# Pairing the level scores of the first mixer behind two rows of the next head's products

## The chip, the cores and the metric

The kernel runs on one core of a Trainium2 chip. The metric is device time in microseconds (us) of one launch. The engines are TensorE (PE: matmuls, PEld: its weight loads), VectorE (DVE), ScalarE (ACT), GpSimd (POOL) and SyncE (SP, which issues the weight loads). Each engine works through its own queue in order and waits on semaphores for the others.

## The reference, cut to what matters

Two blocks of a transformer-like model on 512 tokens of width 1024 in float32: mixers (a gated linear recurrence, sparse attention, dense attention, a long convolution), each followed by a gated feed-forward part. The change lies in the first mixer, which has 8 heads of 128:

```python
def hgrn2_mixer(x, w_in, w_out, gate_norm, lower_bound):
    proj = x @ w_in
    q, f, i, g = jnp.split(proj, 4, axis=-1)
    forget = lb + (1.0 - lb) * jax.nn.sigmoid(f32)
    log_f = jnp.log(jnp.maximum(forget, TINY))
    k = (1.0 - lb) * jax.nn.sigmoid(-f32)
    ...
        decay = jnp.where(causal, jnp.exp(jnp.where(causal, diff, 0.0)), 0.0)
        scores = jnp.einsum('bhtd,bhsd,bhtsd->bhts', qb, kb, decay)
        o = jnp.einsum('bhts,bhsv->bhtv', scores, ib) + ...
    ...
    o = o * lax.rsqrt(jnp.mean(o * o, axis=-1, keepdims=True) + EPS) * gate_norm
    o = o * jax.nn.silu(g)
    return o.reshape(B, L, D_MODEL) @ w_out
```

So for each head: gates and queries from a product with the input, decayed scores between every query and every earlier key, the scores times the values, a norm over the head, a gate.

## The kernel before, in words

The program is written out by hand, one queue for each engine, with semaphores between them. In the first mixer the decays are not built as differences. The 512 tokens are cut in levels n = 0 to 8: at level n a block of 2^n keys meets the next block of 2^n queries, and the decay between them splits in a product over one side and a product over the other. For every head and level VectorE makes one tile `H.E` of decayed keys and queries (`level`, L2181) and updates the running products for the next level (L2189). TensorE multiplies that tile with itself (`scores`). The result in PSUM is collected into `H.S` by mask (VectorE, L2203 and L2206, for levels 0 to 3 and the diagonal) or by copies (ScalarE, L1588, for levels 4 to 6, and L1594 into `H.SO` for 7 and 8).

The order of one head's ten scores is `ORDER = [0, 1, 2, 3, None, 4, 5, 6, 7, 8]`, where `None` is the diagonal, a product of keys and queries without a level. There are four level tiles (`NE = 4`, so level n of a head may be written once the score four levels back has read its tile) and four PSUM banks for scores, `LEVEL_BANKS`, taken in turn.

Between its scores TensorE runs the products of the next head, gate and query, by rows: `head(h + 1, (row,))` is one row k of 8 of the weight tile. It has 6 matmuls of 128x128 by 128x512, since every float32 product is made of three products of rounded parts (L573, L574, L575) and there are two column groups. These rows are cover for VectorE's work. Row 0 of the head after next is done after score 8, then come `values(h)` (L910 to L918), and the next head begins with row 1. So heads 1 to 6 have seven rows and ten scores. The sums of squares of the head before (`head_sums`, L631) stand behind score 3 and the spread of its norm (`head_spread`, L932) behind score 6. Head 7 has no next head: from its sixth score on, rows of the output projection (`mixed`) stand between the scores, which need parts made by ScalarE (L1579) and GpSimd (L2719).

VectorE's queue for a head, in order: clamp of the forget gate (L2226), levels 0, 1, 2 each with its update, collect score 0, level 3, collect 1, collect 2, the low part of a weight tile (L1975), level 4, collect 3, the reciprocal for the norm of the head before (L1988), level 5, collect the diagonal, level 6, level 7, the head before's output (L2213), level 8, the head before's normalisation (L2218), the next head's clamp. That is `LAG = 2`: a score is collected two levels behind the level being made. ScalarE makes the next head's gates and query (L1550 to L1561) after it has collected score 4, and copies the weight tile's high part (L1404) at the end of a head.

Of the kernel before, what the change touches and what calls it, by code (L numbers as in the profile page):

```python
# [17 lines left out]
NT = D // 128  # L18
# [15 lines left out]
LEVEL_BANKS = (2, 4, 5, 6)  # L34
ORDER = [0, 1, 2, 3, None, 4, 5, 6, 7, 8]
# [28 lines left out]
def level_slot(h, n):  # L64

    return (9 * h + n) % NE
# [190 lines left out]
class Signals:  # L257
# [6 lines left out]
    def mark(self, name, *events, by=1):  # L264
        self.total[name] = self.total.get(name, 0) + by
        for event in events:
            self.value[event] = (name, self.total[name])
        self.newest[name.split("_")[0]] = (name, self.total[name])
        return (self.handles[name] if self.handles else None), by
# [4 lines left out]
    def at(self, *event):  # L274
        if self.counted is None:
            return None, 0
        name, value = self.counted[event]
        return self.handles[name], value
# [86 lines left out]
def build(nc, A, out):  # L365
    ctx = ExitStack()
    with ctx:
# [190 lines left out]
        def pe_program(pe):  # L558
# [3 lines left out]
            def wait_bank(b):  # L562
                for event in freed[b] or ():
                    pe.wait_ge(*at(*event))
# [17 lines left out]
            def project(sem, key, banks, done, then, tile=None, ready=None, rows=None, cols=(0, 1)):  # L582

                it = items[key]
                a, b = w_views(it)
                tile = tile or (lambda k: (hh[:, k, :], hl[:, k, :]))
                rows = rows or range(it["kt"])
                wait_weights(key)
                if rows[0] == 0:
                    for j in cols:  # L590
                        wait_bank(banks[j])
                for k in rows:
                    for event in ready(k):
                        pe.wait_ge(*at(*event))
                    for j in cols:
                        bk = banks[j]
                        c = slice(128 * j, 128 * j + 128)
                        last = k == it["kt"] - 1
                        m = product(ps[bk][:, :], [((a[:, k, c], b[:, k, c]), tile(k))], k == 0, last)
                        if last:  # L600
                            m.then_inc(*mark(sem, done[j], *([("used", key)] if j == 1 else [])))
                            freed[bk] = then[j]
# [236 lines left out]
            def hgrn():  # L839
# [4 lines left out]
                for c in range(2):  # L844
# [3 lines left out]
                    for part in range(2):  # L848
# [3 lines left out]
                        for i in range(4):  # L852
                            k = 4 * part + i
# [15 lines left out]
                def head(h, rows):  # L869
                    project("pe_hgrn", ("hgrn", "fq", h), (0, 1), [("f_mm", h), ("q_mm", h)], [[("k_raw", h)], [("q", h)]], ready=ready, rows=rows)  # L870

                def scores(h, n, bk):
                    wait_bank(bk)
                    i = h % 2
                    if n is None:
                        pe.wait_ge(*at("q", h))
                        pe.wait_ge(*at("k", h))
                        a_, b_ = H.K[i], H.Q[i]
                    else:
                        pe.wait_ge(*at("level", h, n))  # L880
                        a_ = b_ = H.E[level_slot(h, n)]
                    if n == 8:
                        for t in range(2):
                            m = pe.matmul(ps[bk][:, 256 * t:256 * t + 256], a_[:, 128 * t:128 * t + 128], b_[:, 256:512], start=True, stop=True)
                    elif n == 7:
                        for t in range(2):
                            m = pe.matmul(ps[bk][:, 128 * t:128 * t + 128], a_[:, 256 * t:256 * t + 128],
                                          b_[:, 256 * t + 128:256 * t + 256], start=True, stop=True)
                    elif n == 6:
                        for t in range(4):  # L890
                            keys, queries = slice(128 * t, 128 * t + 64), slice(128 * t + 64, 128 * t + 128)
                            m = pe.matmul(ps[bk][0:64, queries], a_[:, keys], b_[:, queries], start=True, stop=True)
                    else:
                        for t in range(4):
                            for e in range(2):
                                c = slice(128 * t + 64 * e, 128 * t + 64 * e + 64)
                                m = pe.matmul(ps[bk][64 * e:64 * e + 64, c], a_[:, c], b_[:, c], start=True, stop=True, skip_group_check=True)
                    m.then_inc(*mark("pe_level", ("scores", h, n)))
                    freed[bk] = [("collect", h, n)]

                def values(h):
                    i, hc = h % 2, slice(128 * h, 128 * h + 128)
                    wait_bank(OB)
                    for c in range(2):
                        for tt in range(4):
                            pe.wait_ge(*at("i", c, tt))
                    pe.wait_ge(*at("collect", h, 7))
                    pe.wait_ge(*at("collect", h, 8))
                    for s in range(2):
                        pe.matmul(ps[OB][:, 256:512], H.I[:, s, hc], H.SO[:, 256 * s:256 * s + 256], start=s == 0, stop=False, **kw)  # L910
                    pe.matmul(ps[OB][:, 128:256], H.I[:, 0, hc], H.SO[:, 512:640], start=False, stop=False, **kw)
                    pe.matmul(ps[OB][:, 384:512], H.I[:, 2, hc], H.SO[:, 640:768], start=False, stop=False, **kw).then_inc(
                        *mark("pe_hgrn", ("far_used", h)))
                    pe.wait_ge(*at("collect", h, None))
                    pe.wait_ge(*at("collect", h, 6))
                    for tt in range(4):
                        c = slice(128 * tt, 128 * tt + 128)
                        m = pe.matmul(ps[OB][:, c], H.I[:, tt, hc], H.S[i][:, c], start=False, stop=tt == 3, **kw)  # L918
                    m.then_inc(*mark("pe_hgrn", ("o_mm", h)))
                    freed[OB] = [("o", h)]  # L920

                def head_sums(h):
                    wait_bank(HB)
                    pe.wait_ge(*at("o2", h))
                    sums(HB, sq[h % 2], True, True).then_inc(*mark("pe_hgrn", ("o2_sum", h)))

                    freed[HB] = [("rms", "head", h)]

                def head_spread(h):
                    pe.wait_ge(*at("diagonal", h))  # L930
                    wait_bank(HB)
                    pe.matmul(ps[HB][:, :], ones[:, :], rb[1][:, :], start=True, stop=True).then_inc(*mark("pe_stat", ("spread", "head", h)))  # L932
                    freed[HB] = [("m", h)]

                def mixed(n, rows):

                    project("pe_hgrn", ("hgrn", "out", n), ((0, 1), (4, 5))[n], None, None, ready=mix, rows=rows)

                head(0, None)
                n_level = 0  # L940
                for h in range(8):
                    for i, n in enumerate(ORDER):

                        row = i + (h > 0)
                        if h < 7 and row < NT:
                            head(h + 1, (row,))
                        elif h == 7 and i >= 5:
                            mixed(0, (i - 5,))
                        scores(h, n, LEVEL_BANKS[n_level % 4])
                        n_level += 1  # L950
                        if i == 3 and h:
                            head_sums(h - 1)
                        if i == 7 and h:
                            head_spread(h - 1)
                    if h < 6:
                        head(h + 2, (0,))
                    elif h == 7:
                        mixed(0, (5,))
                    values(h)
# [412 lines left out]
            end("pe", "begin")  # L1372
            normalise("hgrn", 0)
            hgrn()
            ffn(0)
            dsa()
# [1591 lines left out]
```

## Time and profile before

| | |
|---|---|
| median of 3 runs | 2756.11 us (2754.98 to 2756.7) |
| the profiled execution, its own time | 2755.34 us |
| its span, first to last instruction | 2753.4 us |
| granted TensorE clock, mean | 0.996 |
| TensorE, VectorE, ScalarE, GpSimd busy | 2704.0, 1732.6, 1031.1, 136.5 us |

The profile gives for every instruction its start and its duration. Durations of TensorE's matmuls are modelled and overlap, so the distance from one start to the next is what an instruction costs there. "Idle before" is the time for which an engine stood still, with the instruction that released it as inferred from the semaphores.

### The profile page before, as it was taken

Reading aid. Unit: us, or ns where it says so; the run is one execution under the profiler, and the core shown is the slowest. Engines: PE = TensorE matmul, PEld = TensorE weight load, DVE = VectorE, ACT = ScalarE, POOL = GpSimd, SP = SyncE. Lnnn points to the kernel's source line nnn. Section 1 sums busy time; section 2 is a strip of 40 time slices with the busy share of each in tenths; the row PEclk is TensorE's granted clock in tenths of the full one; section 3 lists DMA queues with packets and bytes.
Section 4 is the critical chain, followed back from the end, with each engine's and each line's share of the span. In section 5 each row is a group of like instructions: output and inputs, shape, how many; then the busy total and the mean of one; then the engine's idle time right before and its main releaser. Section 6 shows DMA issues by size and latency. Waiting matters only on the chain.

```text
span 2753.4 us, 36096 instructions
## 1 busy us (share of the span) xinstructions
PE 2704.0 (98%) x14724; PEld 2180.2 (79%) x14724; DVE 1732.6 (63%) x2551; ACT 1031.1 (37%) x1496; POOL 136.5 (5%) x171
## 2 busy tenths in 40 slices
PE   8999899999999999999899999999999999999999
PEld 6777688888876788888675788888887888888888
DVE  4388677465587477565657567575664888643434
ACT  4345444232435444232436543232332222432323
POOL 0000200000034200000003200000000000000000
PEclk9999999999999999999999999999999999999999
DMA  5432134343312134343310036454331111332221
GB/s 172 117 75 66 62 127 153 123 145 96 102 62 77 54 127 153 123 145 96 101 62 16 32 119 200 152 188 134 112 120 58 35 35 35 105 120 93 92 85 54
DMA packets 260572, 276.87 MB, mean 101 GB/s; under 512 B 23799, under 2 KB 227063, under 8 KB 260408
## 3 DMA queue, kind: packets, MB, share of 16 engines
q1 hardware_dynamic: 230216, 219.51, 25.3%
q10 hardware_dynamic: 30192, 55.05, 6.3%
q8 instruction: 118, 1.93, 0.3%
q14 instruction: 46, 0.38, 0.0%
HBM read 267.19 MB, written 7.34 MB: 100 GB/s over the span
## 4 chain that ended last, share of the span: by engine, by line
PE 83%; DVE 4%; ACT 2%; issue 1%; ACTq 0%; DVEq 0%
PE ps L573 23%; PE ps L575 23%; PE ps L574 23%; PE ps L1286 3%; PE ps L1318 2%; PE ps L1045 2%; PE ps L1062 1%; PE ps L1243 1%; PE ps L1264 1%; PE ps L1079 1%; PE ps L1151 1%; ACT sb L1404 1%; PE ps L1130 1%; PE ps L631 0%; PE ps L1196 0%
## 5 line engine op out<-in xcount | busy, mean ns | idle before, releaser
L573 PE MATMUL ps<-sb 128*128 128x512 f32 (+2 forms) x3396 | 1276.1, 376 | 10.6 <-DVE sb L2008 2.5
L574 PE MATMUL ps<-sb 128*128 128x512 f32 (+2 forms) x3396 | 1254.8, 369 | 0.0
L575 PE MATMUL ps<-sb 128*128 128x512 f32 (+2 forms) x3396 | 1254.7, 369 | 0.0
L573 PEld LDWEIGHTS ps<-sb 128*128 128x128 f32 x3396 | 640.1, 188 | 139.4 <-issue 26.5
L575 PEld LDWEIGHTS ps<-sb 128*128 128x128 f32 x3396 | 640.2, 189 | 109.7
L574 PEld LDWEIGHTS ps<-sb 128*128 128x128 f32 x3396 | 640.5, 189 | 106.7 <-issue 1.9
L1975 DVE TENSOR_TENSOR sb<-sb 128x2048 fp32r<-128x2048 f32 (+2 forms) x187 | 417.8, 2234 | 318.4 <-ACT sb L1404 318.3
L1404 ACT ACTIVATE sb<-sb 128x2048 fp32r<-128x2048 f32 (+1 forms) x195 | 363.2, 1862 | 268.7 <-PE ps L575 267.2
L2261 DVE SCALAR_TENSOR_TENSOR sb<-ps,sb 128x511 f32<-128x511 f32 (+1 forms) x264 | 193.5, 747 | 125.8 <-ACT sb L1659 120.6
L1659 ACT ACTIVATE sb<-ps,sb 128x512 f32<-128x512 f32 x132 | 96.1, 778 | 273.5 <-PE ps L575 270.4
L2297 DVE SCALAR_TENSOR_TENSOR sb<-sb 128x512 f32<-128x512 f32 x168 | 126.0, 750 | 13.9 <-DVE sb L2297 0.9
L1690 ACT ACTIVATE sb<-sb 128x512 fp32r<-128x512 f32 x88 | 55.3, 633 | 210.2 <-DVE sb L2319 125.9
L1286 PE MATMUL ps<-sb 128*128 128x256 f32 x512 | 113.5, 380 | 1.3 <-ACT sb L1875 1.3
L1286 PEld LDWEIGHTS ps<-sb 128*128 128x128 f32 x512 | 97.0, 190 | 17.9 <-issue 3.3
L2762 POOL TENSOR_SCALAR sb<-sb 128x512 f32<-128x512 f32 (+3 forms) x128 | 77.1, 616 | 628.0 <-DVE sb L2351 628.0
L2120 DVE SCALAR_TENSOR_TENSOR sb<-ps,sb 128x512 f32<-128x512 f32 x56 | 40.4, 750 | 105.7 <-PE ps L575 105.7
L2118 DVE TENSOR_TENSOR sb<-sb,ps 128x512 f32<-128x512 f32 x58 | 39.1, 685 | 87.2 <-PE ps L575 87.2
L1675 ACT ACTIVATE sb<-sb 128x512 f32<-128x512 f32 x88 | 55.3, 632 | 93.9 <-DVE sb L2261 93.8
L1473 ACT ACTIVATE sb<-sb 128x512 f32<-128x512 f32 x58 | 36.3, 643 | 119.0 <-DVE sb L2079 50.7
L1984 DVE TENSOR_TENSOR sb<-sb 128x512 fp32r<-128x512 f32 x97 | 65.4, 689 | 5.7 <-ACT sb L1889 1.3
L2725 POOL TENSOR_TENSOR sb<-sb 128x2048 fp32r<-128x2048 f32 x8 | 36.9, 4607 | 503.7 <-ACT sb L1404 503.7
L1988 DVE RECIPROCAL sb<-sb 64x128 f32<-64x128 f32 (+4 forms) x36 | 29.7, 825 | 50.3 <-ACT sb L1412 25.3
(239 smaller groups left out, 2202.5 us busy)
## 6 DMA issues: line engine op xcount, KB each, us to landing
sb<-in_ffn_w_up SPq DMA_DIRECT2D x88, 1024.0 KB, 4.9
sb<-in_ada_w ACTq DMA_DIRECT2D x192, 256.0 KB, 3.2
sb<-in_ffn_w_down SPq DMA_DIRECT2D x32, 1024.0 KB, 5.0
sb<-in_ffn_w_down SPq DMA_DIRECT2D x16, 768.0 KB, 4.3
sb<-in_hy_w_in SPq DMA_DIRECT2D x12, 1024.0 KB, 4.9
sb<-in_hgrn_w_in SPq DMA_DIRECT2D x8, 1024.0 KB, 6.3
sb<-in_hgrn_w_in SPq DMA_DIRECT2D x16, 512.0 KB, 4.6
sb<-in_dsa_w_in SPq DMA_DIRECT2D x6, 1024.0 KB, 5.1
```

The source lines that it names most:

```text
L573: pe.matmul(o, al, bh, start=f, stop=False, **kw)
L574: pe.matmul(o, ah, bl, start=False, stop=False, **kw)
L575: m = pe.matmul(o, ah, bh, start=False, stop=l, **kw)
L1286: m = pe.matmul(o, fwm[:, kt, cols], sdz(i, sc)[:, 2 * half + kt, :], start=kt == 0, stop=kt == 1)
L1404: act.activation(wh[w][:, 0:n], raw[it["r"]][:, 0:n], ACTF.Copy).then_inc(*mark("act_hi", ("hi", it["key"])))
L1659: act.activation(dst[:, :], ps[b][:, :], ACTF.Identity, bias=bias(tile), scale=wt(offset, tile)).then_inc(*mark("act_ffn", (name + "_0", n ...
L1675: act.activation(N.sg[i][:, :], N.yg[i][:, :], ACTF.Silu).then_inc(*mark("act_ffn", ("silu", n, t)))
L1975: dve.tensor_tensor(wl[w][:, 0:n], raw[it["r"]][:, 0:n], wh[w][:, 0:n].bitcast(F), SUB).then_inc(*mark("dve_lo", ("lo", it["key"])))
L1984: dve.tensor_tensor(dst, src, high.bitcast(F), SUB).then_inc(*mark(sem, (*name, "lo")))
L2261: dve.scalar_tensor_tensor(o, i, cv[0](tap, tile), o, MUL, ADD).then_inc(*mark("dve_ffn", (name, n, tile) if last else (name + "_1", n, ti ...
L2297: m = dve.scalar_tensor_tensor(a, w[:, :], cact[:, f:f + 1], a, MUL, ADD)
L2762: pool.tensor_scalar(P, P, M.rs[:, c:c + 1], 1.0, MUL, MUL).then_inc(*mark(f"pool_{stage}", ("scaled", stage, u, e)))
```

## The change

The ten scores of a head are taken two at a time. In front of a pair stand the rows that stood in front of each of the two before. Head_sums stays behind score 3, head_spread behind score 6. No instruction is added or taken out, and only TensorE's queue changes.

```diff
                 for h in range(8):
-                    for i, n in enumerate(ORDER):
-
-                        row = i + (h > 0)
-                        if h < 7 and row < NT:
-                            head(h + 1, (row,))
-                        elif h == 7 and i >= 5:
-                            mixed(0, (i - 5,))
-                        scores(h, n, LEVEL_BANKS[n_level % 4])
-                        n_level += 1
-                        if i == 3 and h:
+                    for i in range(0, len(ORDER), 2):
+                        for k in (i, i + 1):
+                            row = k + (h > 0)
+                            if h < 7 and row < NT:
+                                head(h + 1, (row,))
+                            elif h == 7 and k >= 5:
+                                mixed(0, (k - 5,))
+                        for n in ORDER[i:i + 2]:
+                            scores(h, n, LEVEL_BANKS[n_level % 4])
+                            n_level += 1
+                        if i == 2 and h:
                             head_sums(h - 1)
-                        if i == 7 and h:
+                        if i == 6 and h:
                             head_spread(h - 1)
                     if h < 6:
                         head(h + 2, (0,))
```

## Rows read from the trace of the kernel before

**Rows 1.** The page: busy us (share of the span) xinstructions

```profile
PE 2704.0 (98%) x14724; PEld 2180.2 (79%) x14724; DVE 1732.6 (63%) x2551; ACT 1031.1 (37%) x1496; POOL 136.5 (5%) x171
```

**Rows 2.** Windows of heads 1 and 6: length, busy by engine, clock, DMA

```profile
152.00:174.90 22.90, 22.28 (x205) 16.68 (x204) 19.64 (x28) 12.48 (x25) 0.53 (x1) 1.00 0.34 75
...
243.50:266.40 22.90, 22.27 (x205) 16.68 (x204) 19.83 (x28) 12.48 (x25) 0.53 (x1) 1.00 0.15 47
```

**Rows 3.** Timeline, TensorE, head 2: start us, us, engine line op [idle before <-releaser]

```profile
174.91 0.48 PE L573 MATMUL ps<-sb 128*128 128x512 f32 x1
...
176.48 0.69 PE L897 MATMUL ps<-sb 128*64 128x64 f32 x16
177.10 0.50 PE L573 MATMUL ps<-sb 128*128 128x512 f32 x1
...
178.69 0.69 PE L897 MATMUL ps<-sb 128*64 128x64 f32 x16
...
180.90 0.69 PE L897 MATMUL ps<-sb 128*64 128x64 f32 x16
...
183.72 0.42 PE L631 MATMUL ps<-sb 128*32 128x128 f32 x8
184.07 0.50 PE L573 MATMUL ps<-sb 128*128 128x512 f32 x1
...
190.08 0.69 PE L897 MATMUL ps<-sb 128*64 128x64 f32 x16
190.59 0.63 PE L892 MATMUL ps<-sb 128*64 128x64 f32 x8
191.15 1.12 PE L932 MATMUL ps<-sb 128*128 128x512 f32 x2
192.11 0.61 PE L887 MATMUL ps<-sb 128*128 128x128 f32 x4
193.35 1.10 PE L884 MATMUL ps<-sb 128*128 128x256 f32 x4 [0.63 <-ACT sb L1559]
...
197.78 0.48 PE L573 MATMUL ps<-sb 128*128 128x512 f32 x1
```

**Rows 4.** Timeline, VectorE, the same head

```profile
177.22 0.69 DVE L2203 TENSOR_TENSOR sb<-ps,sb 128x512 f32<-128x512 f32 x1 [0.96 <-PE ps L897]
...
179.42 0.75 DVE L2206 COPY_PREDICATED sb<-sb,ps 128x512 f32<-128x512 uint32 x1 [0.19 <-PE ps L897]
181.63 0.74 DVE L2206 COPY_PREDICATED sb<-sb,ps 128x512 f32<-128x512 uint32 x1 [1.46 <-PE ps L897]
182.26 2.27 DVE L1975 TENSOR_TENSOR sb<-sb 128x2048 fp32r<-128x2048 f32 x1
...
192.52 0.68 DVE L2181 TENSOR_TENSOR sb<-sb 128x512 f32<-128x512 f32 x1
...
193.72 0.42 DVE L2226 TENSOR_SCALAR sb<-sb 128x512 f32<-128x512 f32 x1
```

**Rows 5.** Timeline, TensorE, first matmuls of half rows in succession, first and last of four

```profile
315.61 0.40 PE L573 MATMUL ps<-sb 128*128 128x512 f32 x1
...
317.67 0.39 PE L573 MATMUL ps<-sb 128*128 128x512 f32 x1
```

**Rows 6.** Timeline, TensorE, head 7: scores 0, 1 and 2 with nothing between them

```profile
289.40 1.62 PE L897 MATMUL ps<-sb 128*64 128x64 f32 x48
```

**Rows 7.** Timeline, head 0: VectorE's collections 1 and 2, TensorE's score 8

```profile
136.21 1.58 DVE L2206 COPY_PREDICATED sb<-sb,ps 128x512 f32<-128x512 uint32 x2
...
147.49 1.10 PE L884 MATMUL ps<-sb 128*128 128x256 f32 x4 [0.30 <-DVE sb L2181]
```

**Rows 8.** Timeline, ScalarE, head 2: the scaled forget gate of head 3

```profile
192.40 0.83 ACT L1559 ACTIVATE sb<-sb 128x512 f32<-128x512 f32 x1
```

**Rows 9.** Timeline, TensorE, head 7: first row of the output projection, score 6

```profile
294.51 0.47 PE L573 MATMUL ps<-sb 128*128 128x512 f32 x1 [1.01 <-POOL sb L2719]
...
303.08 0.65 PE L892 MATMUL ps<-sb 128*64 128x64 f32 x8 [1.11 <-DVE sb L2181]
```

## The prediction, made before the changed kernel ran

> **What bounds the kernel now.** I began with the page. TensorE is busy for 98% of the span [rows 1], which says little, since starts and not busy times tell where its queue is held. So I cut the eight heads of the first mixer out of the trace: heads 1 to 6 take about 22.87 us each, with TensorE busy 22.3 us and VectorE 19.6 to 19.8 us in such a window [rows 2]. Two engines that are both nearly full, and feed each other, need the order of time. Times in one head are counted from T, the start of its first row (174.91 in head 2; 197.78 in head 3, so the period is 22.87) [rows 3].
>
> TensorE: row, s0, row, s1, row, s2 and so on, one pair of row and score every 2.21 us. (s0 to s3, sN, s4 to s8 are the ten scores in the order of ORDER; sN is the one without a level.) Near the end of the head it stands still for 0.63 us before s8 (193.35) [rows 3]. The row names a ScalarE instruction as releaser, but s8 waits for its level on VectorE, which ended at 192.52 + 0.68 = 193.20 [rows 4], and for a bank long collected. VectorE: it waits three times, for s0 (0.96), s1 (0.19) and s2 (1.46), each time in order to collect the score, and from the collection of s2 at 181.63 to level 8 at 192.52 it never waits [rows 4].
>
> That gives a loop through both engines, which the reader can add up:
> - T to s2, TensorE: 180.90 - 174.91 = 5.99
> - s2 to its collection, 181.63 - 180.90 = 0.73
> - VectorE's own queue from there to level 8: 192.52 - 181.63 = 10.89 (the 2.27 us low part of a weight tile, levels 4 to 7 with their updates, two collections, a reciprocal, the head's output)
> - level 8 to s8: 193.35 - 192.52 = 0.83
> - s8, the row for the head after next, the values, next T: 197.78 - 193.35 = 4.43
>
> Sum 22.87, the whole period. So of TensorE's queue only what lies between s8 and s2 is on the path. From s2 to s8 it is ahead of VectorE.
>
> **The change part by part.** No instruction is added or removed, and no DMA is issued elsewhere. What moves are scores against rows. In heads 1 to 6 before: row 1, s0, row 2, s1, row 3, s2, row 4, s3. After: rows 1, 2, s0, s1, rows 3, 4, s2, s3. Ahead of s2 stand four rows where three stood, and one change from score to row and back is gone.
>
> A second row directly behind a row: three half rows in succession take 317.67 - 315.61 = 2.06, 0.687 each, so a row adds 1.37 [rows 5]. A score to its row is 0.62 (176.48 to 177.10), a row to its score 1.57 to 1.59 [rows 3]. A score directly behind a score: the three at 289.40 take 1.62 together, one alone 0.69, so the step is (1.62 - 0.69) / 2 = 0.46 [rows 6, 3]. One merge therefore saves (1.59 - 1.37) + (0.62 - 0.46) = 0.38.
>
> New times from T: s0 at 1.57 + 1.37 = 2.94 (was 1.57). s1 at 3.40 (was 3.78). Row 3 at 4.02. s2 at 4.02 + 1.59 + 1.37 = 6.98 (was 5.99). s2 is 0.99 later, 1.37 for the row less 0.38 for the merge.
>
> VectorE on the other side: collection of s0 at 3.68 instead of 2.31, level 3, its update, then the collection of s1 (179.42 less its wait of 0.19, less 177.22, is 2.01 later: 5.69 [rows 4]), and the next collection could start 0.85 after that (two take 1.58 together and one 0.73 [rows 7, 4]), near 6.5. s2 is there only at 6.98 + 0.73 = 7.71. So the collection of s2 moves from 6.72 to 7.71, by the whole 0.99. VectorE's waits become about 2.3, 0 and 1.3 where they were 0.96, 0.19 and 1.46. Behind that collection, in VectorE's queue, stands everything down to level 8, and s8, the values and the next T wait for that. Level 3 is late too, but s3 is not asked for before 7.4.
>
> The new period is 7.71 + 10.89 + 0.83 + 4.43 = 23.86: 0.99 more in each of heads 1 to 6.
>
> What TensorE gains behind s2 goes nowhere. Without waits it would now reach s8 after 2.94 + 0.46 + 0.62 + 2.96 + 0.46 for s3, 0.62 + 0.35 for the sums, 2.96 for rows 5 and 6, 0.46 + 0.62, 1.59 for row 7, 0.51 + 0.56 for s5 and s6 (190.08 to 190.59 to 191.15), 0.96 for the spread and 0.45 for s7: 16.5. VectorE lets s8 go at 7.71 + 10.89 + 0.83 = 19.4. The wait ahead of s5 to s8 grows from under 1 us to almost 3. The other queues hold: ScalarE's work for the next head hangs on VectorE's reciprocal and on collected scores, so it shifts with VectorE; its scaled forget gate ends at 192.40 + 0.83 = 193.23 and the clamp that reads it starts at 193.72 [rows 8, 4], 0.5 us of room as before. The sums come before the reciprocal by 4 us. The spread, behind s6 as before, is ready near T + 17.7 (level 6, 16.05 for s6, 0.56, 1.12) and its reader, the next in VectorE's queue after level 8, starts at T + 19.2. Four level buffers and four banks: level 4 needs s0 read, which is long past.
>
> Head 0: VectorE runs there without a wait for TensorE from level 0 to level 8, and s8 waits 0.30 for it [rows 7]. The new s2 comes at about 135.9 (s1 held back by level 1 to 132.3), its collection could start at 136.6, and VectorE gets to it near 137.0 anyway. Nothing lost; the last row ends 1.4 us earlier, and ScalarE's next head starts a few tenths earlier, worth 0.1 at the values (they waited a tenth or two for ScalarE). Head 7 has no next head: s0 to s3 stay in one piece. sN and s4 go behind the first row of the output projection, which waits for GpSimd until 294.51; s5 goes behind two rows, to about 300.1, but s6 has waited for VectorE until 303.08 (1.11) and still does [rows 9]. After it two rows come in one, whose neighbours s7 and s8 cost next to nothing to switch. I take 0 there.
>
> Sum: 6 x 0.99 - 0.1 = +5.84 us. The profiled execution took 2755.34 (span 2753.4 and 1.9 around it), 0.8 below the median of 2756.11; on the median it is 2761.9. After this stage TensorE is full and weight loads have room, so the loss is kept to the end.
>
> Bounds of the unshown: the two orders row, row and score, score are not seen side by side in this stage. If a score behind a score cost as much as one ahead of a row, and the change of work saved nothing, the loss were 1.37 a head, 8.2 in all (2764.3). If rows and scores merge as seen elsewhere, 0.99. I take this, since both spacings have rows of their own. Below: a merge cannot save more than all that a score adds to a row, 2.21 - 1.37 = 0.84, as if the score itself cost nothing: 0.53 a head, 3.2 in all (2759.2).
>
> **Rivals.** First, the other sign: the changes between row and score are the price on the path. Heads 1 to 6 lose 3 of them each, head 0 4, head 7 2: 24 x 0.38 = 9.1 us, 2747.0. For it speaks TensorE's 98% and that it waits so little per head. Against it: TensorE does wait for VectorE before s8 in every head. It decides only if VectorE's stretch from the collection of s2 to level 8 were at least 1 us shorter than 10.89; nothing in the change shortens it. The Trainium skill, TensorEngine Tiling (Array Packing), section Key Properties, says that changing the tiling mode drains TensorE; the scores use 64-column tiles and the rows full ones, and the 0.38 at each merge agrees. By that rule alone the change should give about 9 us, and the skill speaks for it.
>
> Second, nothing: VectorE's idle time (2.6 us a head) absorbs the later scores. It would need the collection of s2 to start as early as before, so s2 no later than 5.99 after T. Against it: the wait for s2, 1.46, is the longest, so s2 is late already. It could hold in part, if the period has slack that I do not see: below +5.5, 2757 to 2761.6.
>
> Third, worse: a pair of scores overtakes VectorE and starts a wait of its own, for instance the spread behind s6 late for the normalisation, or ScalarE's collection of level 4 late. Margins are 1.5 and 0.5 us; if the half-microsecond went, some 0.5 a head more, 2765.
>
> **Chances.** 0.2% is 5.5 us, about what a measurement of this kernel can tell from no change, and my sum is only 0.3 above it. The loop as summed: 0.72, 2760.8 to 2763.2; 0.50 of it above the bound and 0.22 below. Worse: 0.10. Nothing or a small part: 0.10. Faster: 0.08. So slower 0.60, same 0.32, faster 0.08. The range leaves out the faster case and the tails: 2757.5 to 2765.5.
>
> **What would show it.** Periods of heads 1 to 6 near 23.86 (T to T). Score s2 at T + 6.98. VectorE waiting near 2.3 us for s0, none for s1, 1.3 for s2, and 10.89 from there to level 8. TensorE's waits for VectorE before s6, s7 and s8 nearly 3 us a head. Head 0 and head 7 as long as before. I am wrong if s8 no longer waits for level 8, if the stretch of 10.89 changes, or if T to s2 is not 0.99 longer.

## The result and the profile after

The changed kernel takes 2762.61 us (median of 10 runs, 2760.57 to 2765.74), the kernel before 2755.94 in the same measurement. The ratio is 1.0026, 95% interval 1.0017 to 1.0035: slower by some 7 us. A second measurement, on another occasion, gave 2761.35 against 2755.52 and 1.0025 (1.0016 to 1.0034). The profiled execution took 2765.06 (span 2763.2), one of the slower ones of the ten.

The timeline of TensorE in head 2 of the changed kernel answers to [rows 3]. The columns are start us, us, engine, line, operation, count, idle time ahead and its releaser. Groups of x32 are two scores in one.

```profile
177.07 0.48 PE L573 MATMUL ps<-sb 128*128 128x512 f32 x1
...
179.99 1.15 PE L897 MATMUL ps<-sb 128*64 128x64 f32 x32
181.07 0.50 PE L573 MATMUL ps<-sb 128*128 128x512 f32 x1
...
184.02 1.15 PE L897 MATMUL ps<-sb 128*64 128x64 f32 x32
...
191.17 0.69 PE L897 MATMUL ps<-sb 128*64 128x64 f32 x16
193.10 0.65 PE L892 MATMUL ps<-sb 128*64 128x64 f32 x8 [1.24 <-DVE sb L2182]
193.68 1.13 PE L932 MATMUL ps<-sb 128*128 128x512 f32 x2
194.64 0.61 PE L887 MATMUL ps<-sb 128*128 128x128 f32 x4
196.48 1.10 PE L884 MATMUL ps<-sb 128*128 128x256 f32 x4 [1.23 <-ACT sb L1560]
...
200.93 0.48 PE L573 MATMUL ps<-sb 128*128 128x512 f32 x1
```

T is again the start of a head's first row. The period is 200.93 - 177.07 = 23.86 us, against 22.87. T to s2 is 184.02 - 177.07 = 6.95, against 5.99. TensorE stands still for 1.24 ahead of s6 and 1.23 ahead of s8, where it stood 0.63 ahead of s8 alone. These figures count from the modelled end of the matmul before. By starts the waits are a little longer: s7 to s8 is 1.84 us here and was 1.24, and where nothing is waited for it is 0.44 (one pair only, below).

VectorE in the same head, answering to [rows 4] (its lines are one higher than before, since the program grew by a line):

```profile
180.72 0.69 DVE L2204 TENSOR_TENSOR sb<-ps,sb 128x512 f32<-128x512 f32 x1 [2.30 <-PE ps L897]
...
182.66 0.73 DVE L2207 COPY_PREDICATED sb<-sb,ps 128x512 f32<-128x512 uint32 x1
184.75 0.74 DVE L2207 COPY_PREDICATED sb<-sb,ps 128x512 f32<-128x512 uint32 x1 [1.36 <-PE ps L897]
185.38 2.28 DVE L1976 TENSOR_TENSOR sb<-sb 128x2048 fp32r<-128x2048 f32 x1
...
195.65 0.68 DVE L2182 TENSOR_TENSOR sb<-sb 128x512 f32<-128x512 f32 x1
```

It waits 2.30 for s0, not at all for s1, 1.36 for s2. From the collection of s2 to level 8 it needs 195.65 - 184.75 = 10.90 with no wait, as before (10.89).

Head 7 shows something else. Its first row of the output projection comes at 301.66, and then:

```profile
307.24 0.69 PE L897 MATMUL ps<-sb 128*64 128x64 f32 x16
310.23 1.09 PE L892 MATMUL ps<-sb 128*64 128x64 f32 x8 [2.31 <-DVE sb L2182]
311.25 2.08 PE L932 MATMUL ps<-sb 128*128 128x512 f32 x2
312.34 1.25 PE L573 MATMUL ps<-sb 128*128 128x512 f32 x1
```

Score 6 (L892) took 0.65 in [rows 9], here 1.09. The windows over these microseconds (length, busy time by engine, granted clock, DMA share, GB/s) say why:

```profile
306.00:308.00 2.00, 1.92 (x22) 1.30 (x20) 1.97 (x2) 1.10 (x3) 2.00 (x3) 1.00 0.00 0
308.00:310.00 2.00, 0.00 (x0) 0.00 (x0) 2.00 (x3) 0.79 (x4) 1.54 (x1) 0.96 0.00 0
310.00:311.00 1.00, 0.77 (x7) 0.80 (x8) 0.93 (x3) 0.54 (x3) 0.00 (x0) 0.50 0.00 0
...
312.00:313.00 1.00, 1.00 (x3) 0.34 (x1) 1.00 (x3) 0.00 (x0) 0.00 (x0) 0.50 0.00 0
313.00:314.00 1.00, 1.00 (x5) 0.76 (x4) 1.00 (x2) 0.00 (x0) 0.00 (x0) 0.87 0.06 16
```

TensorE had stood still for 2.31 us, and the granted clock was 0.50, the 1.2 GHz level, from 310 until after 313. From s6 to the values head 7 took 318.64 - 310.23 = 8.41 us. In the kernel before it was 7.01 (from 303.08 in [rows 9] to a start at 310.09). This cost 1.4 us in this execution.

### The profile page after: what moved, and what is told of

Its sections match the earlier page's. It is cut to its first block, busy times and chain, and to the rows that moved or that the text cites. A ratio compares the mean times of both kernels' runs of the same rounds, so it can differ in the third digit from the quotient of the medians.

```text
span 2763.2 us, 36096 instructions
## 1 busy us (share of the span) xinstructions
PE 2701.5 (98%) x14724; PEld 2185.2 (79%) x14724; DVE 1733.8 (63%) x2551; ACT 1030.6 (37%) x1496; POOL 136.2 (5%) x171
## 4 chain that ended last, share of the span: by engine, by line
PE 83%; DVE 3%; ACT 2%; issue 1%; ACTq 0%; DVEq 0%
PE ps L573 23%; PE ps L575 22%; PE ps L574 22%; PE ps L1287 3%; PE ps L1319 2%; PE ps L1046 2%; PE ps L1244 1%; PE ps L1063 1%; PE ps L1265 1%; PE ps L1080 1%; PE ps L1152 1%; ACT sb L1405 1%; PE ps L1131 1%; PE ps L631 0%; PE ps L1157 0%
```

## The experiments

The edits, all but one, are to the order in which TensorE takes rows and scores in one head. They are shown with a helper `plan(h)` that gives pairs (rows, scores). `single` is the order before, `paired` that of the change. Row numbers are those of the eight rows of the next head's products; in head 7 they stand for rows of the output projection. The sums stay behind s3 and the spread behind s6.

```python
single = [((i + (h > 0),), (n,)) for i, n in enumerate(ORDER)]
paired = [((i + (h > 0), i + 1 + (h > 0)), ORDER[i:i + 2]) for i in range(0, 10, 2)]
```

The medians, each beside runs of the kernel before on the same chip:

| run | us | before | ratio and interval | period of heads 1 to 5 | head 7 |
|---|---|---|---|---|---|
| changed kernel | 2762.61 | 2755.94 | 1.0026 (1.0017 to 1.0035) | 23.86 to 23.90 | 24.38 |
| the same again | 2761.35 | 2755.52 | 1.0025 (1.0016 to 1.0034) | 23.86 to 23.88 | 22.96 |
| early pairs only | 2762.0 | 2755.68 | 1.0023 (1.0014 to 1.0032) | 23.87 to 23.88 | 22.95 |
| late pairs only | 2756.59 | 2755.68 | 1.0006 (0.9997 to 1.0015) | 22.87 to 22.90 | 22.95 |
| head 7 in the old order | 2761.65 | 2755.68 | 1.0022 (1.0013 to 1.0031) | 23.87 to 23.88 | 22.98 |
| the same again | 2762.21 | 2755.52 | 1.0022 (1.0013 to 1.0032) | 23.86 to 23.88 | 22.99 |
| low part earlier | 2753.87 | 2755.68 | 0.9994 (0.9985 to 1.0003) | 22.61 to 22.65 | 22.96 |
| one pair only | 2750.44 | 2756.03 | 0.998 (0.9971 to 0.9989) | 22.01 | 23.24 |
| few rows early | 2745.88 | 2756.03 | 0.9962 (0.995 to 0.9975) | 21.25 to 21.27 | 22.95 |
| s0 first | 2745.64 | 2755.52 | 0.9968 (0.9955 to 0.998) | 21.35 to 21.38 | 23.24 |

Periods are the distances between the last matmuls of `values` (L918 in the kernel before) of neighbouring heads in the trace. In the kernel before they are 22.86 to 22.88, and head 7 has 22.98. Head 6 is left out because it has no row for a head after next; it took 22.82 before and 23.81 in the changed kernel. With one pair only and with s0 first, head 7 is 0.3 longer, and head 6 is 0.2 shorter than heads 1 to 5 (21.80 and 21.17); why was not followed.

**Early pairs only, late pairs only.** These two halves ask whether a pair costs something, or only its place.

```diff
-                    return paired
+                    return paired[:2] + single[4:]
```

> Only scores 0 to 3 go in pairs (rows 1, 2, s0, s1, rows 3, 4, s2, s3), sN to s8 stand behind single rows as before. My theory, that only what stands between T and s2 is on the path, expects the whole loss of heads 1 to 6: period 23.86, 6 x 0.99 = +5.9 us, 2761.9, and no clock lowered in head 7. The rival, that a pair costs something by itself wherever it stands, expects 2 of 5 pairs' share of the measured +6.7: +2.7 us, 2758.6.

```diff
-                    return paired
+                    return single[:4] + paired[2:]
```

> Scores 0 to 3 behind single rows as before, sN to s8 in pairs. My theory expects the period of heads 1 to 6 at 22.87 as before, T to s2 at 5.99, and longer waits of TensorE ahead of s6 and s8; in head 7 the longer standstill ahead of s6 lowers the granted clock and costs about 1.4 us as in the changed kernel. Together +1.4 us, 2757.3. The rival (each pair costs the same) expects 3 of 5 pairs' share: +4.0, 2759.9. A second rival, that TensorE's switches are the price, expects a gain of some 3 us.

The early pairs alone lose it all: 2762.0, and period 23.87. The late pairs leave the period where it was, 22.87 to 22.90, and the whole cannot be told from no change (1.0006, interval 0.9997 to 1.0015). TensorE with the late pairs only, in head 2:

```profile
174.37 0.47 PE L573 MATMUL ps<-sb 128*128 128x512 f32 x1
...
180.35 0.69 PE L897 MATMUL ps<-sb 128*64 128x64 f32 x16
...
192.80 1.10 PE L884 MATMUL ps<-sb 128*128 128x256 f32 x4 [1.01 <-ACT sb L1565]
...
197.24 0.47 PE L573 MATMUL ps<-sb 128*128 128x512 f32 x1
```

T to s2 is 5.98 again. The one merge among the late scores (sN with s4; s5 and s6 were neighbours before) saves 0.38, and that is what the wait ahead of s8 has grown by, 1.01 where it was 0.63. The rival of a price on each pair expected 2758.6 for the early and 2759.9 for the late pairs and is out. So is the one in which the switches (the changes between rows and scores) are the price, which expected a gain here. The 1.4 us in head 7 did not come, but in this profile a lowered clock cost as much in another place: the values of head 6 took 2.05 where they take 1.10, and head 6 took 24.38 where it had 22.82.

```profile
286.56 2.05 PE L910 MATMUL ps<-sb 128*128 128x256 f32 x4 [1.08 <-ACT sb L1600]
```

The clock was lowered in head 7 of this profile as well, and there it cost nothing:

```profile
296.00:300.00 4.00, 4.00 (x39) 3.07 (x38) 3.99 (x4) 2.63 (x7) 4.00 (x3) 0.57 0.00 0
```

This stretch lies ahead of the wait for VectorE at s6. TensorE arrived later and waited 0.80 there instead of 1.11, and head 7 took 22.95.

**Head 7 in the old order.**

```diff
-                    return paired
+                    return paired if h < 7 else single
```

> The changed kernel with head 7 alone back in the old order. My theory expects +5.9 us (6 x 0.99), 2761.9, with the granted clock at full rate through head 7, and about 1.4 us less than the changed kernel in the profiled head 7. The rival, that the lowered clock in head 7 comes by chance and not from the longer standstill ahead of s6, expects no difference to the changed kernel in the times.

2761.65, with head 7 at 22.98 in its profile. To set it beside the changed kernel on one chip, both ran once more:

> The changed kernel once more, to have a second profile of head 7 and times beside the next run on one chip. If the lowered clock in head 7 belongs to the changed order, the profile shows it there again (head 7 near 24.4 us instead of 22.95) and the time is 1.4 us above the run with head 7 in the old order. If it depends on where in time the standstill falls, head 7 may be near 22.9 here, and the mean of the times lies between 0 and 1.4 us above.

> The kernel with head 7 in the old order once more, on the same chip as the changed kernel: head 7 at 22.95 us, heads 1 to 6 at 23.87, time 2761.7.

The changed kernel gave 2761.35 and its head 7 was 22.96 this time; the one with the old order in head 7 gave 2762.21. TensorE stood as long ahead of s6 in the new profile of the changed kernel, but the clock stayed:

The timeline and the window of that profile:

```profile
309.52 0.65 PE L892 MATMUL ps<-sb 128*64 128x64 f32 x8 [2.30 <-DVE sb L2182]
```

```profile
308.00:314.00 6.00, 4.47 (x24) 3.46 (x25) 5.26 (x8) 1.69 (x7) 0.83 (x1) 1.00 0.01 3
```

So my expectation that head 7's lowered clock belongs to the new order and costs 1.4 us each time was wrong. The same standstill of 2.3 us lowered it in one execution and not in the other, and the two kernels' medians stand in either order (2761.35 and 2762.21). What decides it stays open.

**The low part of the weight tile earlier.** TensorE's order is that of the change. Only VectorE's queue differs.

```diff
+                            if k == 3 and h < 7:
+                                ahead(("hgrn", "fq", h))
                             collect(h, ORDER[k - LAG])
...
-                        if k == 4 and h < 7:
-                            ahead(("hgrn", "fq", h))
```

> The changed kernel's TensorE order, but VectorE does the low part of the weight tile (2.27 us) ahead of the collection of s1 and s2, where it now waits for TensorE, instead of behind it. My theory expects the collection of s2 at T + 8.6 and level 4 at T + 9.25 instead of T + 10.5, so a period of 22.6 us (1.25 less than 23.86), 6 x -0.26 against before, with head 7's 1.4 us about 2755.8. If the pairs cost TensorE time by themselves, the period stays at 23.86 and the time at 2762.6.

2753.87, and the period fell to 22.61 to 22.65 (expected 22.6), with TensorE's work untouched. The time expected was 2755.8; that held 1.4 us for head 7, which took 22.96 and lost nothing. VectorE in head 2:

```profile
177.85 0.69 DVE L2209 TENSOR_TENSOR sb<-ps,sb 128x512 f32<-128x512 f32 x1 [2.31 <-PE ps L897]
...
179.79 2.28 DVE L1981 TENSOR_TENSOR sb<-sb 128x2048 fp32r<-128x2048 f32 x1
181.99 1.60 DVE L2212 COPY_PREDICATED sb<-sb,ps 128x512 f32<-128x512 uint32 x2
```

The low part now stands where VectorE waited for s2, and no wait is left there. Level 4 starts at 183.47 - 174.18 = 9.29 after T instead of 187.57 - 177.07 = 10.50. This is the sharpest of the tests, since it shortens the period from the other side of the loop: what the late score costs runs through VectorE's queue behind it, not through TensorE's. The same move on the old order was not run, so the test shows what bounds the changed kernel, and not that the 1.25 us are to be had only with the pairs.

**Few rows early, and one pair only.** If only rows ahead of s2 cost, all five pairs can stay when the rows go behind it.

```diff
-                    return paired
+                    if h == 0 or h == 7:
+                        return single
+                    return [((1,), (0, 1)), ((2,), (2, 3)), ((3, 4, 5), (None, 4)), ((6, 7), (5, 6)), ((), (7, 8))]
```

> Heads 1 to 6 keep all five pairs, but fewer rows stand in front of the early ones: row 1, s0, s1, row 2, s2, s3, rows 3, 4, 5, sN, s4, rows 6, 7, s5, s6, s7, s8. Heads 0 and 7 as before. My theory: s2 at T + 4.24, its collection when VectorE gets to it at T + 5.08 instead of 6.72, so a period of 5.08 + 10.89 + 0.83 + 4.43 = 21.23 (TensorE alone would need 20.93): 6 x -1.64 = -9.8 us, 2746.1. The rival, that pairs cost by themselves, expects a time above 2756.

```diff
-                    return paired
+                    if h == 0 or h == 7:
+                        return single
+                    return [((1,), (0, 1)), ((2,), (2,)), ((3,), (3,)), ((4,), (None,)), ((5,), (4,)), ((6,), (5,)), ((7,), (6,)), ((), (7, 8))]
```

> Heads 1 to 6 as before but with s0 and s1 together behind row 1, so each later score has one row less in front of it; heads 0 and 7 as before. My theory: VectorE's loop would allow 21.23, TensorE with only two of the switches gone (s1, and s8 behind s7 as before) needs 17.6 to s8 and 4.43 more, 22.0. So the period is 22.0 and bound by TensorE: 6 x -0.87 = -5.2 us, 2750.7. If the position of s2 alone sets the period, with no TensorE bound, it is 21.23 and 2746.1; if a pair costs by itself, above 2755.9.

2745.88 (expected 2746.1) and 2750.44 (expected 2750.7): both beat the kernel before, and with the periods foreseen, 21.25 and 22.01. With few rows early TensorE has s2 directly behind row 2, and VectorE collects s1 and s2 without a wait (the group of two):

```profile
173.89 0.47 PE L573 MATMUL ps<-sb 128*128 128x512 f32 x1
...
175.45 1.15 PE L897 MATMUL ps<-sb 128*64 128x64 f32 x32
...
178.13 1.15 PE L897 MATMUL ps<-sb 128*64 128x64 f32 x32
...
189.94 0.61 PE L887 MATMUL ps<-sb 128*128 128x128 f32 x4
190.71 1.10 PE L884 MATMUL ps<-sb 128*128 128x256 f32 x4 [0.16 <-ACT sb L1567]
...
195.15 0.48 PE L573 MATMUL ps<-sb 128*128 128x512 f32 x1
```

```profile
176.19 0.69 DVE L2211 TENSOR_TENSOR sb<-ps,sb 128x512 f32<-128x512 f32 x1 [0.96 <-PE ps L897]
...
178.12 1.59 DVE L2214 COPY_PREDICATED sb<-sb,ps 128x512 f32<-128x512 uint32 x2
```

T to s2 is 178.13 - 173.89 = 4.24, TensorE waits 0.16 ahead of s8, VectorE 0.96 in the whole head. With one pair only TensorE waits nowhere in the head; VectorE does, for s0 and for the spread, which comes behind the seventh row:

```profile
176.26 0.69 DVE L2211 TENSOR_TENSOR sb<-ps,sb 128x512 f32<-128x512 f32 x1 [0.83 <-PE ps L897]
191.43 0.69 DVE L2226 TENSOR_TENSOR sb<-sb,ps 128x512 f32<-128x512 f32 x1 [0.79 <-PE ps L932]
```

TensorE's s7 and s8 in the same head:

```profile
191.16 0.61 PE L887 MATMUL ps<-sb 128*128 128x128 f32 x4
191.60 1.03 PE L884 MATMUL ps<-sb 128*128 128x256 f32 x4
```

From s7 to s8 TensorE needs 191.60 - 191.16 = 0.44 when it waits for nothing; with few rows early it takes 0.77, so 0.33 of that is a wait.

One pair only has no fewer switches than the kernel before: s1 lost its row, but s6 got one. Its 0.86 us a head come from the earlier s2, which takes away TensorE's wait (0.80 by starts in the kernel before, 1.24 - 0.44). With few rows early three merges more are made (s2 with s3, sN with s4, s5 with s6), 3 x 0.38 = 1.14. They show in TensorE's own time to s8: 191.60 - 173.96 = 17.64 with one pair, and 190.71 - 173.89 - 0.33 = 16.49 with few rows early, 1.15 less. The period falls by 0.76 only, since VectorE then sets the bound.

**s0 first.** The last edit moves s0 ahead of every row, so that VectorE need not wait for it either.

```diff
-                    return paired
+                    if h == 0 or h == 7:
+                        return single
+                    return [((), (0,)), ((1,), (1, 2)), ((2, 3), (3, None)), ((4, 5), (4, 5)), ((6, 7), (6,)), ((), (7, 8))]
```

> Heads 1 to 6: s0 directly behind the values, row 1, s1, s2, rows 2, 3, s3, sN, rows 4, 5, s4, s5, rows 6, 7, s6, s7, s8. VectorE would then collect s2 at about T + 4.1 and its loop would need about 20.3 us a head. My theory: TensorE, with as many switches as in the run with few rows ahead of the early pairs, needs 20.9 and becomes the bound: 6 x (20.9 - 22.87) = -11.8 us, 2744.1, and VectorE waits while TensorE hardly does. If VectorE were still the bound at 21.25, the time would be 2746 as in that run; if TensorE had no bound, 6 x -2.6, 2740.4.

2745.64, nothing gained on few rows early, with period 21.35 instead of 20.9. The time is that of the rival in which VectorE is still the bound (2746), but the trace speaks against it: TensorE has no wait in the head and VectorE waits 1.05 for the spread, so the bound did go to TensorE. The size was off because I had left out switches. s0 by itself adds 0.79 between the values and row 1 (0.99 + 0.61, less the 0.81 from values to row), where it adds 0.46 beside s1. And the sums now stand between two scores that could have been merged (178.81 to 179.78, 0.97 from s3 to sN against 0.46; the sums themselves are 0.35 of that). Together these are 0.49, for the 0.45 by which the period was missed. TensorE, and then VectorE ahead of the normalisation:

```profile
178.81 0.69 PE L897 MATMUL ps<-sb 128*64 128x64 f32 x16
179.42 0.43 PE L631 MATMUL ps<-sb 128*32 128x128 f32 x8
179.78 0.69 PE L897 MATMUL ps<-sb 128*64 128x64 f32 x16
```

```profile
189.22 0.69 DVE L2226 TENSOR_TENSOR sb<-sb,ps 128x512 f32<-128x512 f32 x1 [1.05 <-PE ps L932]
```

## Why the prediction was right

- **The loop through both engines.** It was the bound. Period foreseen 23.86, measured 23.86 in head 2; over heads 1 to 6 the trace has 143.18 us where it had 137.17, 1.00 a head for the 0.99 of the sum. The halves, one pair only and the low part of the weight tile show that it is the place of s2 and what VectorE has behind it.
- **A row 1.37, a merge 0.38.** T to s2 foreseen 6.98, measured 6.95. From the start of s0 to the next row is 181.07 - 179.99 = 1.08 for two scores, as 0.46 + 0.62 had it.
- **VectorE's waits** foreseen 2.3, 0 and 1.3, measured 2.30, 0 and 1.36, and 10.90 behind them.
- **TensorE's gain behind s2 goes nowhere.** Shown by the late pairs only: same period, a longer wait ahead of s8. The waits ahead of s6 and s8, foreseen at almost 3, are 1.24 + 1.23 = 2.47 as the rows give them; by starts they are 2.82 (193.10 - 191.17 less the 0.51 of an s5 to s6 without a wait, and 1.84 less 0.44).
- **Heads 0 and 7 at nothing.** Head 0, from its first row of the next head's products to the last product of its values, took 152.02 - 128.23 = 23.79 us before and 153.17 - 129.47 = 23.70 after. Head 7 took 22.98 before, and 22.96 in the second profile. In the first it lost 1.4 to a lowered clock, which none of my cases held. It is in some executions only.
- **The size.** +5.84 foreseen on the median, +6.67 and +5.83 measured in two sets. That the second agrees to 0.01 is luck, as its interval runs from 4.4 to 9.4 us; the periods are the evidence. The profiled execution is 9.8 us longer in span: 6.0 in heads 1 to 6, 1.4 in head 7, 1.2 that was there before head 1 began (153.17 against 152.02), and the rest after the stage. The second profile of the changed kernel shows the last two, and head 7's, to differ between executions of one kernel. Its span is 2757.6, shorter by 5.6: 1.4 in head 7, 0.7 ahead of head 1, and 3.5 behind the stage. There the first profile has a granted clock of 0.76 over 805 to 812 us and 0.79 over 1464 to 1480, where the second has 1.00 in both.
- **The rival of the other sign** named its condition, VectorE's stretch 1 us shorter. The run with the low part earlier took 2.2 us out of that stretch and put them ahead of it, where VectorE had waited, 1.25 us less in all. Against the kernel before beside it, it was 1.8 us lower where the changed kernel was 5.8 to 6.7 higher, level with the kernel before (0.9985 to 1.0003). By the Trainium skill, TensorEngine Tiling (Array Packing), Key Properties, a change of tiling mode drains TensorE; the 0.38 a merge agrees with that. No run separates a drain from the other differences between rows and scores. The 0.38 became time only where TensorE was the bound: from one pair only to few rows early, 0.76 of 1.14 us a head.
- **The other two rivals.** VectorE's idle time absorbed nothing: the period grew by all that s2 was late. And no pair started a wait of its own, since in head 2 VectorE's normalisation and clamp follow level 8 without a wait (196.25 and 196.85 behind 195.65).

## What to carry to other kernels

Where two engines feed each other, add up the loop through both, from one wait to the same wait one round later, before pricing a change: an edit that makes one engine cheaper loses time if it puts more work ahead of the item that the other engine is waiting for. A saving in switches is collected by moving the filler behind that item: here the same five pairs cost 6 us or gave 10, by which rows stand in front of the first two (in the second case with heads 0 and 7 in the old order). And when a loop is bound by one engine's queue, look what in that queue waits for nothing and could fill its idle time ahead of the critical item.

## What the runs showed of the hardware

A standstill of TensorE of 2.3 us ahead of s6 was followed by a granted clock of 0.50 for some 3 us in one profile of the changed kernel and by none in another (1.00 over 308 to 314 us), with the same instructions and the same wait. It cost 1.4 us. With the late pairs only, waits of 1.02 ahead of s8 and 1.08 ahead of the values of head 6 were followed by it as well (L910 at 2.05 for 1.10); the changed kernel has waits of 1.23 and 1.09 in these two places, and none followed there (L910 at 1.10).

What a lowered clock costs depends on where it falls. In head 7 a stretch of it ahead of s6, for which TensorE waits anyway, cost nothing: 0.57 over 296 to 300 us with the late pairs only, 0.52 over 293 to 296.5 with the low part earlier, and head 7 took 22.95 and 22.96. Behind that wait it cost the 1.4 us.

A change worth a few us has this in its spread: runs of the changed kernel lay between 2759.4, at a mean granted clock of 0.996, and 2765.7, at 0.992.
